# Homes of their own for decode's first keys and queries, output weights cast beside its last exponentials, and identity products in TensorE's waits

## What is computed

```
def mla_sample(x, ckv_pool, kpe_pool, page_table, w_dq, g_q, w_uq, w_dkv, g_kv, w_uk, w_uv, w_o):
    q_nope, q_pe, c_kv, k_pe = mla_project(x, pos, w_dq, g_q, w_uq, w_dkv, g_kv)
    ckv_past = ckv_pool[page_table].reshape(B, past, MLA_KV_LORA)
    kpe_past = kpe_pool[page_table].reshape(B, past, MLA_ROPE)
    q_lat = jnp.einsum("bthn,chn->bthc", q_nope, w_uk)
    s_past = jnp.einsum("bthc,bkc->bhtk", q_lat, ckv_past) + jnp.einsum("bthr,bkr->bhtk", q_pe, kpe_past)
    ...
    p = jax.nn.softmax(s, axis=-1).astype(c_kv.dtype)
    o_lat = jnp.einsum("bhtk,bkc->bthc", p[..., :past], ckv_past) + jnp.einsum("bhtk,bkc->bthc", p[..., past:], c_kv)
    o = jnp.einsum("bthc,chv->bthv", o_lat, w_uv).reshape(B, T, MLA_HEADS * MLA_VDIM)
    return o @ w_o, c_kv, k_pe
```

## Time and profile before

| | us |
|---|---|
| three runs | 1556.83, 1558.58, 1561.95 |
| median | 1558.58 |
| the profiled execution | 1557.15 |
| its span | 1555.3 |
| TensorE busy (share of the span) | 1458.9 (94%) |
| VectorE busy | 675.7 (43%) |
| ScalarE busy | 466.4 (30%) |
| GpSimd busy | 612.6 (39%) |
| mean granted clock of TensorE | 0.976 |

### The profile page before, as it was taken

The page is one execution under the profiler, slowest core; times in us unless marked ns, Lnnn a source line. Parts: engine busy times, 40 slices in busy tenths (PEclk is TensorE's granted clock), DMA queues, the critical chain, the costliest instruction groups (busy, mean ns, idle before and its releaser), DMA issues.

```text
span 1555.3 us, 28213 instructions
## 1 busy us (share of the span) xinstructions
PE 1458.9 (94%) x12103; PEld 1351.2 (87%) x12103; DVE 675.7 (43%) x984; ACT 466.4 (30%) x866; POOL 612.6 (39%) x276
## 2 busy tenths in 40 slices
PE   6969996888999999999999999998989999999997
PEld 6857773555899999999999999896679999999997
DVE  4668776887254400233113444425666420034112
ACT  5215554333342221222321111113733221122322
POOL 2412223442346643466343443331024563466441
PEclk9979997999999999999999999998999999999999
DMA  4234853785243534444432674467933435434321
GB/s 159 76 102 164 276 188 145 292 302 218 69 150 136 210 142 144 173 169 142 156 137 96 221 250 145 148 213 244 324 109 136 162 136 183 169 135 155 142 81 55
DMA packets 124059, 258.80 MB, mean 166 GB/s; under 512 B 7256, under 2 KB 104680, under 8 KB 117696
## 3 DMA queue, kind: packets, MB, share of 16 engines
q1 hardware_dynamic: 117824, 219.73, 41.3%
q0 software_dynamic: 6144, 37.75, 6.5%
HBM read 249.87 MB, written 95.58 MB: 222 GB/s over the span
## 4 chain that ended last, share of the span: by engine, by line
PE 87%; DVE 7%; issue 2%; ACT 2%; DMA 0%; POOL 0%; SPq 0%; DVEq 0%; ACTq 0%
PE ps L539 23%; PE ps L543 23%; PE ps L540 23%; PE ps L846 4%; PE ps L748 2%; PE ps L1051 1%; PE ps L795 1%; PE ps L867 1%; DVE KT L1567 1%; ACT sc L2277 1%; PE ps L1085 1%; PE ps L763 1%; PE ps L1071 1%; PE ps L952 1%; PE ps L728 1%
## 5 line engine op out<-in xcount | busy, mean ns | idle before, releaser
L2330 POOL TENSOR_TENSOR whl<-wraw,whl 128x2048 fp32r<-128x2048 f32 (+3 forms) x127 | 448.6, 3540 | 540.0 <-ACT whl L1976 540.0
L539 PE MATMUL ps<-hA,whl 128*128 128x260 f32 x1216 | 323.3, 287 | 12.0 <-POOL hA L2330 6.6
L540 PE MATMUL ps<-hA,whl 128*128 128x260 f32 x1216 | 318.6, 283 | 0.0
L1976 ACT ACTIVATE whl<-wraw 128x2048 fp32r<-128x2048 f32 (+3 forms) x127 | 186.1, 1486 | 425.4 <-PE ps L543 387.2
L539 PE MATMUL ps<-uT,whl 128*128 128x260 f32 x1024 | 268.4, 283 | 0.0
L540 PE MATMUL ps<-uT,whl 128*128 128x260 f32 x1024 | 266.3, 281 | 0.0
L543 PE MATMUL ps<-hA,whl 128*128 128x260 f32 x1216 | 247.2, 285 | 0.0
L539 PEld LDWEIGHTS ps<-hA,whl 128*128 128x128 f32 x1216 | 231.3, 190 | 15.2 <-issue 13.3
L540 PEld LDWEIGHTS ps<-hA,whl 128*128 128x128 f32 x1216 | 232.0, 191 | 0.1
L543 PE MATMUL ps<-uT,whl 128*128 128x260 f32 x1024 | 206.8, 283 | 0.0
L540 PEld LDWEIGHTS ps<-uT,whl 128*128 128x128 f32 x1024 | 193.3, 189 | 0.0
(11 more groups left out here) (303 smaller groups left out, 2071.7 us busy)
## 6 DMA issues: line engine op xcount, KB each, us to landing
out_ds<-in_state SPq DMA_DIRECT2D x32, 2047.0 KB, 10.3
wraw<-in_w_up SPq DMA_DIRECT2D x32, 1024.0 KB, 5.6
wraw<-in_w_down SPq DMA_DIRECT2D x32, 1024.0 KB, 5.1
wraw<-in_w_qkv SPq DMA_DIRECT2D x18, 1024.0 KB, 5.3
out_ds<-in_state SPq DMA_DIRECT2D x8, 2044.0 KB, 12.4
dv<-in_state SPq DMA_DIRECT2D x36, 256.0 KB, 5.5
dv<-q_scratch SPq DMA_DIRECT2D x6, 1024.0 KB, 6.8
wraw<-in_w_omla SPq DMA_DIRECT2D x4, 1024.0 KB, 11.4
```

What stands on the lines that cost most here:

```text
L539: pe.matmul(ps[:, 2 * u + a, 0:HALF], hi(k), rhs(k, 0)[:, c], start=first, stop=False)
L540: pe.matmul(ps[:, 2 * u + a, 0:HALF], hi(k), rhs(k, 1)[:, c], start=False, stop=False)
L1976: ins = act.activation(dst(0), src, ACT.Copy)
L2330: return pool.tensor_tensor(dst, src, hi.bitcast(F32), ALU.subtract)
```

## The change

Four things are done.

1. Groups 0 and 1 of the keys are transposed into ring buffers 6 and 7 of `gat` (`keys_at`) and not into `KT`, and `qbd0` gets memory of its own beside `olat`. So VectorE clears `qbd0` and turns groups 0 and 1 ahead of the last `values`, and ScalarE spreads sample 0's queries there. GpSimd issues the gather of group 3 right behind that of group 2; group 6's gather waits for unit 0's scores. Clearing `pfin` moves from before unit 0 to unit 1 on VectorE.
2. ScalarE casts the first output chunk in two pieces of 1024 columns, on both sides of the last `unit_exp`; GpSimd subtracts in the same two pieces.
3. `late_linear` is cut in two calls. The half for columns 260 to 519 runs after `sum_rows` of the last sample, ahead of its `turn_latent`; the other half stays where it was. For this the latent banks 6 and 7 change places.
4. `warm(n, bank)` issues n products of the identity with itself, 128x128 by 512 columns in float32, into a PSUM bank that nobody reads. They stand at ten places of the order, 23 products in all; the output is not touched by them.

VectorE around the start of decode before. The four big transposes are key groups 0 to 3; `tmp<-ps,shareP` takes the last prompt output, `tmp 128x512` clears `pfin`.

The diff, cut to its core:

```
+        def keys_at(n):
+            return gat[:, GR - 2 + n, :] if n < 2 else KT[:, n % KR, :]
...
+            def warm(n, bank):
+                for _ in range(n):
+                    pe.matmul(ps[:, bank, :].rearrange("p (o c) -> p o c", o=4), ident[:],
+                              ident[:].rearrange("p (o c) -> p o c", o=1).to_broadcast([P, 4, P]), start=True, stop=True,
+                              skip_group_check=True)
...
-            def late_linear(sample_split):
+            def late_linear(sample_split, a, us, hi, lo):
+                if a:
+                    pe.wait_ge(tile_low, sample_split - 1)
+                    pe.wait_ge(keys_exp, NU)
+                    pe.wait_ge(latent_taken, NS - 1)
+                else:
+                    pe.wait_ge(tile_low, sample_split)
...
                 pe.wait_ge(tile_taken, vw.at("tile_summed", 2))
+                if lows == 0:
+                    warm(5, 2 * us[0])
                 pe.wait_ge(norm_low, lows + early)
...
                 z_end(pe.transpose(ps[0:n, 2 * u, KVL:KVL + ROPE], kpeT[64:96, tok], ident[64:96, 64:96]))
+                if t in (1, 3):
+                    warm(4 if t == 1 else 1, 2 * u + 1)
...
             for step in range(3):
                 project(step)
+                warm(2 if step < 2 else 1, 4)
...
                     pe.wait_ge(tile_taken, vw.at("tile_summed"))
+                if n == NI + 2:
+                    warm(2, 0)
                 if t == 2 and p:
                     values(p - 1)
...
                     unit_scores(u)
                     spread_max(u)
+                if u == 0:
+                    warm(2, 1)
...
                     sum_rows((u - 2) // 2)
+                if u == NU:
+                    late_units = [(vw.at("tile_summed") + 1 + mt) % 4 for mt in range(2)]
+                    late_parts = wparts(w_begin(), 0, KC, MC)
+                    sample_split = vw.tick("a", DT + 1)
+                    late_linear(sample_split, 1, late_units, *late_parts)
...
+            warm(1, 4)
             pe.wait_ge(spread_in, 16)
             pe.wait_ge(shares_ready, 1)
             for i in range(2):
                 if i:
+                    warm(3, 4)
                     pe.wait_ge(dil_out_taken, DU)
...
+                if n == NI + 1:
+                    dve.memset(qbd0[:], 0.0).then_inc(queries_cleared, 1)
+                    turn_group(0)
+                    turn_group(1)
...
+                if n == NI + 1:
+                    act.wait_ge(queries_cleared, 1)
+                    act.wait_ge(query_copied, 2)
+                    for part_ in range(2):
+                        spread_queries(0, part_)
...
+                if u == NU - 1:
+                    act.wait_ge(unit_scored, NU)
...
+                    act.activation(whl[:, slot_, 0, 0:WC // 2], wraw[:, slot_, 0:WC // 2], ACT.Copy).then_inc(first_half_high, 1)
                 if u < NU:
                     unit_exp(u)
+                if u == NU - 1:
+                    act.activation(whl[:, slot_, 0, WC // 2:], wraw[:, slot_, WC // 2:], ACT.Copy).then_inc(chunk_high, 1)
...
             pool.wait_ge(output_ready, H // 2)
             gather(2)
+            gather(3)
             h_tile(H // 2 - 1, slice(NS, T))
             pool.wait_ge(output_taken, H // 2)
-            for n in range(3, NS * NG):
+            for n in range(4, NS * NG):
+                if n == GR - 2:
+                    pool.wait_ge(unit_scored, 1)
```

More of the change, by code:

```diff
@@ L97, in program @@
         KT = sb("KT", [P, KR, GW], F32, cx)
-        qbd = [sb(f"qbd{i}", [P, 9, 2, 32], F32, cx) for i in range(2)]
+        qbd1 = sb("qbd1", [P, 9, 2, 32], F32, cx)
         cx.close()
@@ L1585, in _ @@
                     if n >= NI:
-                        for i in range(2):
-                            ins = dve.memset(qbd[i][:], 0.0)
-                        ins.then_inc(queries_cleared, 1)
-                        turn_group(0)
+                        dve.memset(qbd1[:], 0.0).then_inc(queries_cleared, 1)
                     dve.wait_ge(turned_taken, TURN["share", p - 1, 0] + 1)
@@ L1600, in _ @@
                     new_bias()
-            turn_group(1)
-            dve.wait_ge(tile_low, vw.at("a"))
-            for i in range(2):
-                dve.memset(pfin[i], 0.0)
+                if n == NI + 1:
+                    dve.memset(qbd0[:], 0.0).then_inc(queries_cleared, 1)
+                    turn_group(0)
+                    turn_group(1)
+            dve.wait_ge(tile_low, vw.at("a") - 1)
             def row_max(u):
@@ L1648, in latent_out @@
                 dve.wait_ge(latent_ready, b + 1)
[L1649 removed]
+                link(dve.tensor_copy(pnb[:], ps[:, 6 + (b + 1) % 2, 2 * H:3 * H]))
                 for k in range(2):
                     ins = dve.scalar_tensor_tensor(out=olat[:, k, :, b], in0=pnb[:], scalar=ckvT[:, k, b:b + 1],
[L1652 removed]
+                                                   in1=ps[:, 6 + (b + 1) % 2, k * H:(k + 1) * H], op0=ALU.mult, op1=ALU.add)
                 ins.then_inc(latent_taken, 1)
             for u in range(NU + 3):
+                if u == 1:
+                    dve.wait_ge(tile_low, vw.at("a"))
+                    for i in range(2):
+                        dve.memset(pfin[i], 0.0)
                 if u < NU - 1:
@@ L2105, in copy_queries, with spread_queries @@
                     ins.then_inc(query_copied, 1)
+            def spread_queries(b, part_):
+                for i in (2 * part_, 2 * part_ + 1):
+                    r = slice(32 * i, 32 * i + 32)
+                    c = slice(H * (i // 2), H * (i // 2 + 1))
+                    act.activation(qbd[b % 2][r, 0:8, i % 2, c], qrep[r, :, :, b], ACT.Copy)
+                    ins = act.activation(qbd[b % 2][r, 8, i % 2, c], qpe[r, :, b], ACT.Copy)
+                ins.then_inc(queries_spread, 1)
             for n in range(NI + 4):
@@ L2178, in latent_copy @@
                 act.activation(latent, ps[:, 4 + b % 2, :], ACT.Copy).then_inc(latent_copied, 1)
-            for b in range(2):
-                for part_ in range(2):
-                    spread_queries(b, part_)
+            for part_ in range(2):
+                spread_queries(1, part_)
             for u in range(NU + 1):
```

50 lines of the change are left out of this document (21 added, 29 removed).

## The result

The changed kernel takes 1546.28 us (median; its runs lie between 1545.47 and 1547.67), the kernel before 1558.8 us on the same chip: ratio 0.9918, interval 0.9902 to 0.9934. The forecast was 1546.9. The profiled execution of the changed kernel took 1547.67 us, 9.5 us under the profiled one of before, while the medians differ by 12.5: before's profile happened to lie 1.7 us under its median, after's 1.4 us over. The traces can account for 9.5.

What follows compares the result with a forecast made beforehand. TensorE, busy 94% of the span, was taken as the bound, leaving its waits and lower-clock stretches. 1.5 + 5.5 + 4.2 + 1.2 - 0.7 = 11.7 us off 1557.15 gives 1545.45, or 1546.9 on the median's scale; range 1541 to 1553.

Steps and rivals of the forecast that it cites:

- First product: Before the first product: five identity products fill the wait and hold the clock; 1.5 us won, bounds 0 and 1.55.
- Latents and first heads: Latents' transposes to first heads: identity products fill gaps and keep TensorE at 2.4 GHz; 5.5 us won, bounds 2.0 and 6.9.
- no window at 0.50 between 90 and 110: Sign of success among projection steps and first heads: no stretch from 90 to 110 us at 1.2 GHz.
- windows at 0.50 stand behind the identity products: Sign that the prediction is wrong: TensorE runs at 1.2 GHz behind the identity products.
- The doubt about 84.7 to 87.4: Latents, 86.2 to 88.9 before: the 1.3 us there was in doubt, as TensorE does little from 81.3 to 86.2.
- Start of decode: Attention's end to unit 2: early keys and queries start unit 0 6.4 us earlier; 4.2 us won, bounds 3.1 and 6.0.
- the 266: Decode's start: sign that the prediction is wrong, if unit 1 waits for group 3 past 266 us.
- this overrun: Between units 0 and 1: two identity products at 1.2 GHz take 3.4 us of a wait of about 2.5.
- End of decode: Split casts and the column half ahead let output products start at 395.6; 1.2 us won, bounds -0.5 and 3.4.
- the warning that the clock falls again in the narrow stretch: Decode's end, 401.3 to 407.4: narrow products and waits may bring back a loss of 2.1 to 2.7 us.
- Merge: Merge of dilated attention: an identity product ahead of the shares' spread delays it; 0.7 us lost, bounds 0 and -0.9.
- The rival of slow identity products: All filled gaps: identity products run at 1.2 GHz, overrun and don't hold the clock; +7.7 us, 1566.3, chance 0.04.

Runs made afterwards that it cites:

- only the front kept: Changed kernel without the eight identity products ahead of the last `values`, behind unit 0 and at the merge; 1545.38 us, ratio 0.9875.
- both halves together: Changed kernel with the output half for columns 260 to 519 put back next to the other half behind decode; 1548.0 us, ratio 0.99.
- output spread: Changed kernel without the merge's identity products, first output half spread in 4, 3 and 9 steps over waits at decode's end; 1544.8 us, ratio 0.9877.
- both ends: Changed kernel without merge products, plus output spread, unit 0's maxima ahead of group 2's turn and seven identity products behind unit 0; 1544.02 us, ratio 0.9876.

## Why the prediction was right, and where it was not

The forecast was right in its sum, and in four of its five terms the trace is within 0.3 us of it.

- *First product*: 1.5 forecast, 1.5 measured.
- *Latents and first heads*: 5.5 forecast, 5.3 by the last scores. The cause is shown from three sides: without the products the stretch is as before, with them alone it is repaired, and with two thirds of them it falls behind the gap left open. The test "no window at 0.50 between 90 and 110" failed: 99.7 to 103.1 reads 0.50. With it came true what was to show the prediction wrong, "windows at 0.50 stand behind the identity products". The products do not hold the clock everywhere; they leave one fall or none where there were three. The doubt about 84.7 to 87.4 was unfounded in this execution (1.00), but not in general: in three kernels with the same fifteen products (only the front kept, both halves together, output spread) 85.0 to 88.4 reads 0.50 to 0.53 and 97.1 to 104.9 reads 1.00. The first scores stand near 98.5 to 98.9 there.
- *Start of decode*: 4.2 forecast, 4.1 measured (10.9 less 6.8). With the 7.0 us expected ahead of it, unit 0 was due at 246.7 and came at 246.57; group 2 at 251.9, turned from 251.97; unit 2 between 265 and 268, at 267.25. Unit 1 was due at 257.7 to 258.8 and came at 259.48, past the 266 (less what was won) that was to show the prediction wrong. It did not wait for group 3's keys, though, which were turned at 258.7. The two identity products ahead of it took 3.76 us at 1.2 GHz and ended behind them. The prediction had named this overrun (3.4 us in a wait of 2.5) and left it out of unit 1's range. By its own figures that range was short by another 0.2: 2 us of queue ahead of group 3's gather would cost 1.3, not 1.1. The experiment with only the front's shows that unit 2 doesn't care.
- *End of decode*: 1.2 forecast, 0.9 in the trace, 0.8 by the experiment. The working held closely (10.9 us earlier than written: `turn_latent` 390.4 and 390.38, second half 396.5 and 396.33), and so did the warning that the clock falls again in the narrow stretch. What it did not see is that the order was the fault: 48 products ahead of the last latent leave the waits behind it empty. Spread over them they bring 4.1 us more.
- *Merge*: -0.7 forecast with a bound of -0.9, and -1.1 measured. The term was mis-sized. The product was priced at its rate in a row of products (0.86); where the next work waits behind it, its start and end count as well (1.12 in the row of L536).
- *Not in the sum*: 1.0 us lost between 415 and 1063. A stretch at 936 runs at 0.53 for longer than before. It was there before, and in two kernels (only the front kept; both ends) it is absent, with 646.2 us from the last output product to the first dilated scores; the others have 647.3 to 648.7. The change has no instruction there, and the changed kernel again, on another chip, has 647.7, as before the change. So this loss is a chance of the one execution.

The rival of slow identity products happened in part, at two places where the clock was down when the gap began, as its condition said; both lay off the path to unit 2. The time was met more closely than the working deserves, and that is luck: the traces give 9.5 us, the medians 12.5, and the forecast's sum was 11.7.

## What to carry to other kernels

Fill a wait with empty products only where real work of the same engine would run at the lower clock behind it, and where the filling ends before the wait does: ahead of finished inputs it is plain delay, and with the clock already down it takes twice as long. Before that, look for real work that can be spread over the waits: at decode's end the stretch took 19.9 us with that work behind the waits, 19.1 with it as one block ahead, and 14.9 with it spread over them. When one wait goes, the next supplier (here the gathers) sets what is won, so work that needs nothing of it belongs ahead of it.

## What the runs showed of the hardware that was not expected

- Transposes held TensorE's clock at 1.00 as products do (15.4 to 21.9 in the kernel with 276 of them). A float32 transpose of 128x128 took 0.112 us in a row of 60.
- With the same fifteen identity products ahead of decode, the clock fell once ahead of 110 us in nine of ten traces, at 85 or at 99, and not at all in the tenth. The place differed between executions on one chip.
- The same loop runs at two paces, 110.3 and 112.8 us from unit 2 to the last unit, by a wait of VectorE for TensorE that is 0.89 or 1.14 us in the same place; the pace went with the chip (first chip, two traces; three others, twelve).
- With four gather DMAs in flight (two groups, latents and rotary part each), the DMA moved about 400 GB/s and a group's rotary part took longer to land. In the changed kernel, windows over all engines (us; busy of PE, PEld, DVE, ACT, POOL; PEclk, DMA share, GB/s):

```profile
250.00:253.00 3.00, 0.67 (x7) 0.17 (x3) 1.03 (x1) 0.55 (x3) 2.63 (x3) 1.00 1.00 404
256.00:259.00 3.00, 3.00 (x4) 0.94 (x4) 2.86 (x3) 0.25 (x1) 2.39 (x3) 0.50 1.02 412
```

  Group 3's, issued between 248.1 and 250.4, landed after 6.6 us, against 4.8 for group 2's in the earlier trace rows.
